# GDN inversion: 16x16 blocks by row substitution on VectorE instead of three doubling levels on TensorE

## The reference

```python
gcum = jnp.cumsum(gc, axis=-1)
decay = jnp.exp(jnp.where(tril, gcum[..., :, None] - gcum[..., None, :], -jnp.inf))
kb = kc * bc[..., None]
a = jnp.where(strict, jnp.einsum('nbhid,nbhjd->nbhij', kb, kc) * decay, 0.0)
ia = a + jnp.eye(lc, dtype=jnp.float32)
u = lax.linalg.triangular_solve(ia, vc * bc[..., None], left_side=True, lower=True, unit_diagonal=True)
w = lax.linalg.triangular_solve(ia, kb * jnp.exp(gcum)[..., None], left_side=True, lower=True,
                                unit_diagonal=True)
```

## Time and profile before

| what | value |
|---|---|
| median of 3 runs | 1892.83 us (1892.53 to 1894.47) |
| profiled execution, its span | 1893.0 us |
| PE busy | 1867.0 us (99%) |
| DVE busy | 1087.0 us (57%) |
| ACT busy | 729.3 us (39%) |
| POOL busy | 223.4 us (12%) |
| GDN stage | about 309 to 698 us of the span |

### The profile page before, as it was taken

How to read it: one execution, slowest core, us unless ns; L and a number is a source line. 1 busy time by engine, 2 the same in 40 slices (tenths; PEclk the granted TensorE clock), 3 DMA queues, 4 the chain that set the end, 5 groups by cost and what they waited for, 6 DMA issues and landing times.

```text
span 1893.0 us, 31005 instructions
## 1 busy us (share of the span) xinstructions
PE 1867.0 (99%) x9409; PEld 1579.4 (83%) x9409; DVE 1087.0 (57%) x2433; ACT 729.3 (39%) x1467; POOL 223.4 (12%) x379
## 2 busy tenths in 40 slices
PE   7999999999999999999999999999999999999997
PEld 6999998888888888888888888888888888888886
DVE  6666666888888874564545454433334444444455
ACT  4444444545444433353333333333333333333330
POOL 2343432222222200001110110000000000000000
PEclk9999999999999999999999999999999999999999
DMA  8666665444444435346555646544444555456541
GB/s 216 168 166 162 161 171 126 109 113 111 114 110 113 116 120 161 94 128 163 157 158 161 172 122 170 162 129 128 129 130 142 150 161 161 127 166 211 162 134 67
DMA packets 317412, 270.76 MB, mean 143 GB/s; under 512 B 96600, under 2 KB 230624, under 8 KB 316704
## 3 DMA queue, kind: packets, MB, share of 16 engines
q1 hardware_dynamic: 306880, 250.90, 47.3%
q0 software_dynamic: 10464, 18.99, 4.1%
HBM read 249.73 MB, written 20.06 MB: 143 GB/s over the span
## 4 chain that ended last, share of the span: by engine, by line
PE 98%; DVE 1%; DMA 0%; issue 0%; SPq 0%; ACT 0%; DVEq 0%; POOL 0%; ACTq 0%; POOLq 0%
PE bank L296 71%; PE bank L2013 9%; PE bank L1749 7%; PE bank L1865 2%; PE bank L1242 1%; PE bank L1224 1%; PE bank L1236 1%; PE bank L1218 1%; PE bank L415 0%; DMA x_res<-in_x_sample 0%; PE bank L638 0%; PE bank L1192 0%; PE bank L1285 0%; PE bank L1214 0%; PE bank L1200 0%
## 5 line engine op out<-in xcount | busy, mean ns | idle before, releaser
L272 DVE TENSOR_TENSOR w_lo<-raw,w_hi 128x512 fp32r<-128x512 f32 (+2 forms) x828 | 562.4, 688 | 620.9 <-ACT w_hi L267 616.8
L267 ACT ACTIVATE w_hi<-raw 128x512 fp32r<-128x512 f32 (+2 forms) x828 | 502.4, 616 | 838.6 <-PE bank L296 703.1
L296 PE MATMUL bank<-w_hi,aT_hi 128*128 128x512 f32 (+2 forms) x1776 | 696.3, 392 | 1.7 <-DVE aT_lo L430 1.6
L296 PE MATMUL bank<-w_hi,aT_lo 128*128 128x512 f32 (+2 forms) x1776 | 673.6, 379 | 0.0
L296 PE MATMUL bank<-w_lo,aT_hi 128*128 128x512 f32 (+2 forms) x1776 | 672.6, 379 | 0.0
L296 PEld LDWEIGHTS bank<-w_hi,aT_hi 128*128 128x128 f32 x1776 | 334.8, 189 | 58.7 <-issue 9.7
L296 PEld LDWEIGHTS bank<-w_hi,aT_lo 128*128 128x128 f32 x1776 | 334.0, 188 | 55.7
L296 PEld LDWEIGHTS bank<-w_lo,aT_hi 128*128 128x128 f32 x1776 | 335.1, 189 | 47.7
L296 PE MATMUL bank<-w_hi,hT_hi 128*128 128x512 f32 x288 | 112.1, 389 | 0.0
L296 PE MATMUL bank<-w_lo,hT_hi 128*128 128x512 f32 x288 | 112.1, 389 | 0.0
L296 PE MATMUL bank<-w_hi,hT_lo 128*128 128x512 f32 x288 | 112.0, 389 | 0.0
(11 more groups left out here) (365 smaller groups left out, 1962.5 us busy)
## 6 DMA issues: line engine op xcount, KB each, us to landing
raw<-in_ffn_w_gate SPq DMA_DIRECT2D x176, 256.0 KB, 2.7
raw<-in_ffn_w_up SPq DMA_DIRECT2D x176, 256.0 KB, 2.7
raw<-in_ffn_w_down SPq DMA_DIRECT2D x176, 256.0 KB, 3.4
raw<-in_w_in SPq DMA_DIRECT2D x128, 192.0 KB, 2.4
raw<-in_w_in SPq DMA_DIRECT2D x128, 128.0 KB, 2.3
raw<-in_w_in SPq DMA_DIRECT2D x256, 64.0 KB, 2.3
raw<-in_w_out SPq DMA_DIRECT2D x61, 256.0 KB, 3.3
h_blocks<-sg SPq DMA_DIRECT2D x11, 768.0 KB, 4.6
```

The source lines that it names most:

```text
L267: nc.scalar.activation(w_hi[:, g % RING, 0:width], raw[:, g % RAW, 0:width], ACT.Copy).then_inc(sem("w_high"), 1)
L272: nc.vector.tensor_tensor(w_lo[:, g % RING, 0:width], raw[:, g % RAW, 0:width], w_hi[:, g % RING, 0:width], ALU.subtract).then_inc(sem("w_ ...
L296: last = nc.tensor.matmul(acc[t][:, 0:width], l[:, k0 + n, t * P:(t + 1) * P], r[:, g % RING, 0:width], start=(n == 0 and j == 0), stop=(n ...
```

## The change

The 16x16 diagonal blocks are inverted on DVE, and levels 1 to 3 go. Levels 4, 5 and 6 stay, for tiles 0 and 1 only. In detail, for each head:

- DVE: instead of `B`, `T`: a product of `A` with a block mask, a reduction of the 128x384 result to the 128x48 diagonal blocks, a copy of the unit rows into `inv`, 15 shuffles that spread row k of each block to all its lanes (`below`), then 15 steps of two operations (a product and a subtraction of 128 x 3 x k), each of which waits for the one before (`after`), and one spreading product into `T`. The transpositions into `U` stay.
- The steps are cut in three parts (`ROWS_AT`, `ROWS_OF`), and the convolutions and silus of q and v are placed between them.
- The root of the key norms goes from DVE to POOL, as 12 dependent operations. The z gate goes from DVE to POOL, as two operations. The nine row DMAs of POOL are issued behind its masks of `decT`.
- The samples' products with the state and what follows from them come at level 4 instead of level 5.

```diff
-LEVEL_AT = (0, 17, 20, 23, 27, 31, 34)
-LEVELS_DONE = 37
+KEYS_AT, NORM_AT, DECAY_AT = 7, 9, 11
+QUERY_AT, QUERY_DONE, VALUE_AT, VALUE_DONE = 13, 16, 20, 22
+ROWS_AT = (14, 17, 20)
+ROWS_OF = (range(BLOCK - 1, 10, -1), range(10, 5, -1), range(5, 0, -1))
+SPREAD_AT = 23
+LEVEL_AT = {4: 25, 5: 28, 6: 32}
+LEVELS_DONE = 36
...
 in gdn_pe:
-                    yield 9
+                    yield KEYS_AT
                     L("g_cv", 1, 3), W("g_mix")
...
-                    yield 16
+                    yield QUERY_DONE + 1
                     L("g_cv", 2, 3)
                     for t in range(TT):
                         last = nc.tensor.transpose(tl(b5, t), tl(gqT, t), ident)
                     last.then_inc(sem("g_tok_ps"), 1)
-                    for n in range(1, LEVELS):
+                    yield VALUE_DONE + 2
+                    L("g_cv", 3, 3)
+                    for t in range(TT):
+                        last = nc.tensor.transpose(tl(b3, t), tl(cv[:, 2, :], t), ident)
+                    last.then_inc(sem("g_tok_ps"), 1)
+                    for n in range(LOW, LEVELS):
...
 in gdn_act:
+                    yield KEYS_AT
                     W("g_decin")
                     nc.scalar.activation(dec[:], dec[:], ACT.Exp).then_inc(sem("g_dec"), 1)
-                    tanh(1)
+                    squares(0, b6, Z)
...
+                    yield QUERY_AT
                     W("g_fall")
                     nc.scalar.activation(decT[:], decT[:], ACT.Exp, scale=-1.0).then_inc(sem("g_decT"), 1)
+                    tanh(1)
+                    yield QUERY_DONE + 1
                     squares(1, b5, qkdT)
+                    yield VALUE_AT
                     tanh(2)
+                    yield VALUE_DONE + 2
+                    L("g_tok_ps", 3, 3), L("g_nrs", ROOT_STEPS, ROOT_STEPS)
...
 in gdn_dve:
+                    yield KEYS_AT
+                    conv(1, range(2))
+                    yield NORM_AT
...
-                    after(V.tensor_tensor(B, A, lv[0].unsqueeze(1).broadcast_to([P, TT, P]), ALU.mult))
-                    V.tensor_tensor(T[:], ident.unsqueeze(1).broadcast_to([P, TT, P]), B, ALU.subtract)\
-                        .then_inc(sem("g_T1"), 1)
-                    W("g_T1")
+                    after(V.tensor_tensor(U[:], A, cn[:, C_SAME:C_SAME + P].unsqueeze(1).broadcast_to([P, TT, P]),
+                                          ALU.mult))
+                    after(V.tensor_reduce(diag.rearrange("p (t c) -> p t c", t=TT),
+                                          U[:].rearrange("p t (g c) -> p t c g", g=GROUPS), AX, ALU.add))
+                    V.tensor_copy(inv, cn[:, C_OWN:C_OWN + BLOCK].unsqueeze(1).broadcast_to([P, TT, BLOCK]))
+                    for k in range(1, BLOCK):
+                        ins = V.stream_shuffle(below[:, k, :], diag,
+                                               [lane // BLOCK * BLOCK + k for lane in range(SQUARE)])
+                    after(ins)
+                    yield QUERY_AT
+                    conv(1, range(2, TAP - 1))
+
+                    def rows(part):
+                        for k in ROWS_OF[part]:
+                            after(V.tensor_tensor(prod[:, :, 0:k], tiles(below[:, k, :])[:, :, 0:k],
+                                                  inv[:, :, k:k + 1].broadcast_to([P, TT, k]), ALU.mult))
+                            after(V.tensor_tensor(inv[:, :, 0:k], inv[:, :, 0:k], prod[:, :, 0:k], ALU.subtract))
+                    yield ROWS_AT[0]
+                    rows(0)
+                    yield QUERY_DONE
+                    silu(1)
+                    yield ROWS_AT[1]
+                    rows(1)
+                    yield VALUE_AT - 2
+                    conv(2, range(TAP - 1))
+                    yield ROWS_AT[2]
+                    rows(2)
+                    yield SPREAD_AT - 1
+                    silu(2)
+                    yield SPREAD_AT
+                    after(V.tensor_tensor(T[:].rearrange("p t (g c) -> p t g c", g=GROUPS),
+                                          inv.unsqueeze(2).broadcast_to([P, TT, GROUPS, BLOCK]),
+                                          cn[:, C_SAME:C_SAME + P].rearrange("p (g c) -> p g c", g=GROUPS).unsqueeze(1)
+                                          .broadcast_to([P, TT, GROUPS, BLOCK]), ALU.mult))
                     V.transpose(U[:, 0, :], T[:, 0, :]).then_inc(sem("g_Ua"), 1)
                     V.transpose(U[:, 1:3, :], T[:, 1:3, :]).then_inc(sem("g_Ub"), 1)
...
-                            rsqrt_rough(nrs[:], nss[:, 1, :], npol[:], after)
...
-                            rsqrt_refined(nrs[:], nss[:, 1, :], npol[:], after)
-                            V.tensor_tensor(nrs[:].unsqueeze(2), nrs[:].unsqueeze(2), bhalf[:, :, bass.ds(h, 1)],
-                                            ALU.mult).then_inc(sem("g_nrs"), 1)
...
 in gdn_pool, root() giving each operation a wait on its own semaphore:
+                    pool_wait(pool, sem("g_own"), G_OWN * h + G_NSS)
+                    x, y, square = nss[:, 1, :], nrs[:], npol[:]
+                    root(G.tensor_scalar(y.bitcast(I32), x.bitcast(I32), -0.5, float(0x5F3759DF), ALU.mult, ALU.add))
...
+                    W("g_thz")
+                    G.tensor_scalar(zg[:], zg[:], 1.0, None, ALU.add).then_inc(sem("g_zg"), 1)
+                    pool_wait(pool, sem("g_zg"), 2 * h + 1)
+                    G.tensor_tensor(zg[:], zg[:], gbuf[:, :, 3 * HD:], ALU.mult).then_inc(sem("g_zg"), 1)
```

More of the change, by code:

```diff
@@ L139, in constants @@
     c[:, C_MS + P:C_MS + 2 * P] = np.where((col <= row) & same, 0, NEG)
[L140 to L143, removed]
+    for n in range(STEPS):
+        s = 1 << LOW + n
+        above = (row // (2 * s) == col // (2 * s)) & (row // s % 2 == 0) & (col // s % 2 == 1)
+        c[:, C_LV + n * P:C_LV + (n + 1) * P] = above
+    c[:, C_SAME:C_SAME + P] = row // BLOCK == col // BLOCK
+    c[:, C_OWN:C_OWN + BLOCK] = row % BLOCK == col[:, 0:BLOCK]
     c[:, C_BM:C_BM + NB] = row // NQ == np.arange(NB)[None, :]
@@ L1237, in gdn_pe @@
                             .then_inc(sem("g_UZa_ps"), 1)
[L1238 to L1243, removed]
-                        if n == 4:
[L1245 to L1250, removed]
+                        L("g_Zb", step, STEPS)
+                        if step > 1:
+                            L("g_Tb", step - 1, STEPS - 1)
+                        nc.tensor.matmul(tl(b7, 2), T[:, 1, :], Z[:, 1, :], start=True, stop=True)\
+                            .then_inc(sem("g_UZb_ps"), 1)
+                        if n == 4:
                             yield LEVEL_AT[n] + 2
@@ L1577, in gdn_pool @@
                             .then_inc(sem("g_pre"), 1)
+                    pool_wait(pool, sem("f_o_ps"), HEADS)
+                    of_pair = kqm.rearrange("p (j a) c -> p j (a c)", a=2)
+                    pool_wait(pool, sem("g_cv"), 3 * h + 1)
+                    for a in range(2):
+                        last = G.tensor_copy(of_pair[:, :, 3 * NQ * a:3 * NQ * a + NQ],
+                                             tl(gkT, 2).rearrange("p (j c) -> p j c", j=4)[:, :, NQ * a:NQ * a + NQ])
@@ new lines, in gdn_pool @@
+                    for c0, c1, c2 in ((1.5, -0.5, 0.0), (1.875, -1.25, 0.375)):
+                        root(G.tensor_tensor(square, y, y, ALU.mult))
+                        root(G.tensor_tensor(square, square, x, ALU.mult))
+                        if c2:
+                            root(G.tensor_scalar(npol2[:], square, c2, c1, ALU.mult, ALU.add))
+                            root(G.tensor_tensor(square, square, npol2[:], ALU.mult))
+                            root(G.tensor_scalar(square, square, c0, None, ALU.add))
+                        else:
+                            root(G.tensor_scalar(square, square, c1, c0, ALU.mult, ALU.add))
+                        root(G.tensor_tensor(y, y, square, ALU.mult))
@@ new lines, in gdn_pool @@
+                    root(G.tensor_tensor(nrs[:].unsqueeze(2), nrs[:].unsqueeze(2), bhalf[:, :, bass.ds(h, 1)], ALU.mult))
+                    pool_wait(pool, sem("g_cv"), 3 * h + 2)
+                    G.tensor_copy(of_pair[:, :, NQ:3 * NQ], tl(gqT, 2).rearrange("p (j c) -> p j c", j=4))\
+                        .then_inc(sem("g_kqm"), 1)
+                    W("g_decT")
+                    for to, m in ((slice(0, 2), C_LP), (slice(2, 3), C_LS)):
+                        x = decT[:, to, :]
+                        last = G.tensor_tensor(x, x, cn[:, m:m + P].unsqueeze(1).broadcast_to(
+                            [P, to.stop - to.start, P]), ALU.mult)
```

159 lines of the change are left out of this document (71 added, 88 removed).

## The result

The changed kernel takes 1952.4 us (median of 4 runs, 1950.32 to 1954.77) against 1893.2 for the kernel before beside it (4 runs, 1892.53 to 1894.47): 1.031 times as long, 95% interval 1.0296 to 1.0325. The forecast was 1931, the range 1914 to 1960. So the sign and the mechanism were forecast, and the loss came out at 59 us in place of 38. The time lies outside the band of 1922 to 1942 to which the forecast gave 63%, in the part that rival 3 had opened. The profiled execution took 1952.95 us, with a span of 1951.3.

A forecast was written before the change was run, and what follows sets the result against it. PE was taken as the bound, with late DVE stopping it: a head of 48.58 - 4.54 + 0.7 + 5.6 + 3.0 gives 53.35 us, 38.2 more for eight heads, so 1931 us; range 1914 to 1960.

The forecast's parts named there:

- rival 3: GDN heads: PE's clock falls to 1.2 GHz in its waits, losing up to 3.4 us a head, 1958 us; 17%.
- What PE saves: Levels 1 to 3 leave PE: 1.80, 1.37 and 1.37, together 4.54 us a head.
- the three waits: PE waits for DVE's silus: 0.7 us at the keys, 5.6 at the q block, 3.0 at the v block.
- What DVE must do: DVE's work in order puts q's silu at 21.2 us into the head and v's at 29.3.
- the walk: The sum of DVE's operations in order through a head, priced from start to start.
- A split takes 0.65: Each DVE split on the way to q's and v's silu was priced at 0.65 us.
- yet before DVE's: ACT's splits, behind the tanh of q and v, come before DVE's; listed under what costs nothing.
- I take 0.60: DVE's strided reduction of 384 elements: 0.60 us, with bounds of 0.60 and 1.2.
- From level 4 to the end: Head's end on PE: 21.93 us plus two slots (1.38), less the v block (0.33), gives 22.98.
- Rival 2: Half the loss is hidden by cheaper shuffles and row steps at 0.16: 2.7 us a head, 1914 us; 7%... 13%.
- What costs nothing: The key norms' root and z gate on POOL, its row DMAs and ACT's splits are covered, adding no time.

The follow-up runs named there:

- qearly: The changed kernel with all of q's convolution, its tanh and silu back ahead of the norm step: 1961.02 us.
- fill: The changed kernel with 24 products whose result nothing reads put ahead of PE's wait at the q block: 1963.62 us.
- norows: The changed kernel with the 30 row operations of each head left out, so the blocks are not inverted: 1928.79 us.
- port: The changed kernel with POOL's mask of the decays moved behind its stores and behind the spread of the blocks: 1945.69 us.
- second form of 8: The change with blocks of 8, levels 3, 4 and 5 in later slots than the first such form, POOL's mask behind the spread: 1913.69 us.
- low3: The change with blocks of 8: levels 3 to 6 on PE, 7 shuffles and 14 row operations on DVE, q's silu early: 1902.42 us.
- pad16: The changed kernel with an unused tile of 16 columns behind the constants tile: 1949.91 us.
- pad112: The changed kernel with an unused tile of 112 columns behind the constants tile: 1939.29 us.
- pad: The changed kernel with an unused tile of 368 columns behind the constants, putting later tiles at their old addresses: 1939.17 us.
- pad48: The changed kernel with an unused tile of 48 columns behind the constants tile: 1939.63 us.
- poolonly: The kernel before with only the key norms' root and the z gate moved to POOL: 1891.13 us.

## Why the forecast was right, and where it was small

**What PE saves, and the three waits.** The steps hold. The keys start at 7.75 (forecast 7.70). PE's wait for q is 6.01 (forecast 5.6), for v 0.61 (3.0). The wait for v was mis-sized because the sum has PE at full clock on the way there; at half clock it is later at the v block by 2.99 us (8.15 us of work in place of 5.16), which the wait absorbs. That 0.61 are left is because DVE's silu came 0.6 later than its sum said, too. The mechanism, a head set by DVE's sum and no longer by PE's, is what *qearly* and *fill* show: the v block stays at 30.12 and 30.55 whatever PE does before it. It is also what *norows* and *port* show from the other side: less time on DVE, and the v block comes sooner.

**What DVE must do: the sum was 1.3 us short.** q block 21.80 for 21.2, v block 30.56 for 29.3, level 4 31.65 for 30.37. Three terms, read against the walk:
- "A split takes 0.65" left out that the split at NORM_AT stands behind ACT's part of it: 0.75 idle at 427.00, 0.67 net of the 0.1 that I had for the completion. ACT's part stands behind its squares and copies of the keys. My sentence that ACT's splits are behind the tanh "yet before DVE's" was wrong there and, in *norows* and the second form of 8, dearer still.
- "I take 0.60" for the reduction: start to start it took 0.85 (429.82 to 430.67), inside the bounds, 0.25 more. The Trainium skill, Vector Engine (DVE) Microarchitecture Reference, section 5.2, gives 1.73 ns a column where one source hops 4 KiB at every element. By it, as an estimate, the duration is 0.16 + 384 x 1.73 ns, 0.82, and the trace has 0.82, though the steps here are 64 bytes. Here the skill's figure would have been a better source than the nearest row. (With groups of 8, *low3*, the same 384 columns took 0.94, more than that figure gives.)
- POOL's mask beside the rows: about 0.6 between the q and the v block, shown by *port*. The forecast counted POOL only as an engine with time to spare, not as a neighbour that slows DVE. The term was left out without a reason.

The shuffles (2.05 for 2.2, both with completion), the row operations (0.24 to 0.20 apart) and the silus came out as priced or a little under, which gives back some 0.2 of these 1.5.

**From level 4 to the end**: 22.45 for 22.98, 0.5 too much. The old 21.93 held small gaps of PE that the new head doesn't have: behind the closing block the next product starts after 0.24 us in place of 0.42, the products T Z of level 4 take 0.59 in place of 0.82, and those of level 6 0.36 in place of 0.46. So a usual head is 54.10 for 53.35, and 0.75 x 8 is 6 us of the miss.

**The clock, rival 3.** It falls in every head, as that rival said, and the part between q and v block is hidden, as it said too. That it falls again in three heads costs 1.6 us each, 5 us. The rival had up to 3.4 in each head; it was a question of how much, not of which. The rule of the Trainium skill that I cited with it, that an idle array is throttled and activity releases it, agrees with the windows above (1.00, then 0.50 late in the wait, and 1.00 again under work).

**The place of the tiles**: +13 us, in no step of mine. The diff showed the constants tile getting shorter; I read that as nothing. Without it the kernel takes 1939, inside my 1922 to 1942. The range covers 1952 only because rival 3 had widened it for another reason, so that part is luck. Against it, 3.7 us were gained ahead of the stage (the first head's copy starts at 305.34 in place of 309.02), where the fall of the earlier trace rows is missing from the trace after:
```profile
68.00:70.00 2.00, 2.00 (x27) 1.79 (x25) 1.21 (x3) 0.52 (x1) 0.14 (x1) 1.00 0.44 108
```
The change is not shown to be the cause. Among the variants with the same FoX code the fall is there in *pad16*, *pad112*, *norows*, *qearly* and both forms of 8 (first copy at 306.3 to 308.7) and missing in *pad*, *pad48*, *fill* and *port* (305.5 to 306.2). What decides it is open. 6 + 5 + 13 - 4 is 20 of the 21 us between 1931 and 1952, and the 4 came by chance as far as the traces show.

**A slip in the range.** Rival 2 takes 1.6 us off the row steps. Thirty operations at its 0.16 are 4.8, which is 1.9 less than the 6.7 of the walk, so its end is 1912 rather than 1914.

**What costs nothing.** Root and z gate on POOL were covered: *poolonly* shows no loss, even a gain of 3 us, and in the changed kernel no wait of PE is for POOL or for what ACT makes of the root.

## What to carry to other kernels

Here one engine was busy for 40 of 48 us in a stage, and some 10 us of dependent work put onto it (reduction, shuffles, rows) made it the bound, however idle it looks on the page of the profile; the shorter list on the old bound bought nothing. So sum the dependent work of a stage by engine before you move work. A wait that you create has a second price in the low clock behind it: look at what PE does in the few us after the wait, and prefer that a product stream hidden anyway stands there. And whenever an edit changes the size of a tile, look at the mean ns of a product that the edit doesn't touch; here the place of the tiles was worth 13 us, a fifth of the whole loss.

## What the runs showed of the hardware

- A 128x512 product with `hT` as its stationary tile takes 389 ns from start to modelled end if the tile is shifted by 0, -1024 or -1280 bytes (multiples of 256) from its old place, and 395 to 396 if it is shifted by 64, -1408 or -1472, with PE never idle and the clock full. In a window of 100 us that is 442 or 443 products against 430 to 432.
- POOL's work on tensors in SBUF can slow DVE's: a row operation of 0.19 us took 0.63 beside POOL's mask, and 0.19 again with the mask elsewhere (*port*); in the second form of 8 a split of 0.69 took 1.23 beside the mask. In *port* DVE's operations beside the moved mask kept their time.
- Fifteen shuffles of 128x48, each with its own mask load, follow each other by 0.123 us although each lasts 0.20; dependent DVE operations of this size follow by 0.20 to 0.24.
- After 6 us of waiting with the q block next, PE's products start 0.43 apart instead of 0.23 for 5 us, and only then at full speed.
